# Feed-forward of a streaming encoder step as Strassen's seven block products

## Time and profile before

| | |
|---|---|
| time, median of 3 runs | 2838.29 us (2837.95 to 2841.03) |
| profiled execution, span | 2834.8 us |
| TensorE busy | 2717.8 us, 96% of the span, 18594 matmuls |
| VectorE busy | 1578.1 us, 56% |
| ScalarE busy | 1007.8 us, 36% |
| feed-forward matmuls L1857 | 6 groups of 768, 128x352 each, from 2081.47 us to the end of the span |

### The profile page before, as it was taken

How to read it: one execution, slowest core, us unless ns; L and a number is a source line. 1 busy time by engine, 2 the same in 40 slices (tenths; PEclk the granted TensorE clock), 3 DMA queues, 4 the chain that set the end, 5 groups by cost and what they waited for, 6 DMA issues and landing times. The chain is left out here.

```text
span 2834.8 us, 47428 instructions
## 1 busy us (share of the span) xinstructions
PE 2717.8 (96%) x18594; PEld 2642.7 (93%) x18594; DVE 1578.1 (56%) x2975; ACT 1007.8 (36%) x2302; POOL 207.6 (7%) x299
## 2 busy tenths in 40 slices
PE   5999989999999999989999989998989999999999
PEld 5999889999999999979999989998989999999999
DVE  5433536566566566557998845454363444444434
ACT  4333336556655656653343422112221111111110
POOL 0000000000000000004555510000000000000000
PEclk8999999999999999999999989999989999999999
DMA  4332353343343343328888854333221111111112
GB/s 161 122 122 76 107 156 101 96 124 101 90 128 104 90 134 97 92 84 193 210 200 211 203 157 141 120 121 125 70 89 45 45 45 45 45 47 54 50 56 97
DMA packets 326606, 308.72 MB, mean 109 GB/s; under 512 B 66480, under 2 KB 283056, under 8 KB 326256
## 3 DMA queue, kind: packets, MB, share of 16 engines
q1 hardware_dynamic: 326384, 305.69, 37.1%
HBM read 218.32 MB, written 87.28 MB: 108 GB/s over the span
## 5 line engine op out<-in xcount | busy, mean ns | idle before, releaser
L411 PE MATMUL banks<-w_hi,xn_hi 128*128 128x256 f32 x1440 | 408.3, 288 | 5.0 <-DVEq L368 5.0
L411 PE MATMUL banks<-w_lo,xn_hi 128*128 128x256 f32 x1440 | 403.4, 284 | 0.0
L414 PE MATMUL banks<-xn_hi,w_hi 128*128 128x352 f32 x1152 | 380.2, 330 | 11.9 <-ACTq L352 7.3
L414 PE MATMUL banks<-xn_hi,w_lo 128*128 128x352 f32 x1152 | 379.6, 330 | 0.0
L414 PE MATMUL banks<-xn_lo,w_hi 128*128 128x352 f32 x1152 | 379.3, 329 | 0.0
L411 PE MATMUL banks<-w_hi,xn_lo 128*128 128x256 f32 x1280 | 364.0, 284 | 0.0
L411 PEld LDWEIGHTS banks<-w_hi,xn_hi 128*128 128x128 f32 x1440 | 274.9, 191 | 6.6 <-DVEq L368 5.1
L411 PEld LDWEIGHTS banks<-w_lo,xn_hi 128*128 128x128 f32 x1440 | 274.5, 191 | 0.1
L1857 PE MATMUL banks<-h_hi,w_hi 128*128 128x352 f32 x768 | 248.9, 324 | 2.5 <-DVEq L1778 2.5
L1857 PE MATMUL banks<-h_hi,w_lo 128*128 128x352 f32 x768 | 248.7, 324 | 0.0
L1857 PE MATMUL banks<-h_lo,w_hi 128*128 128x352 f32 x768 | 248.7, 324 | 0.0
(11 more groups left out here) (282 smaller groups left out, 5903.2 us busy)
## 6 DMA issues: line engine op xcount, KB each, us to landing
w_raw<-in_w_in SPq DMA_DIRECT2D x44, 1024.0 KB, 5.9
scratch_xbc<-att_co SPq DMA_DIRECT2D x32, 512.0 KB, 2.9
ssd_ab<-scratch_acum SPq DMA_DIRECT2D x64, 256.0 KB, 5.9
br_g<-scratch_gates SPq DMA_DIRECT2D x72, 176.0 KB, 3.8
scratch_gates<-hand_tanh SPq DMA_DIRECT2D x48, 176.0 KB, 5.4
att_k<-scratch_k_hi SPq DMA_DIRECT2D x64, 128.0 KB
scratch_z<-att_z_stage SPq DMA_DIRECT2D x64, 128.0 KB, 2.0
ssd_xbc<-scratch_xbc SPq DMA_DIRECT2D x64, 128.0 KB, 3.4
```

The source lines that it names most:

```text
L411: ins = self.nc.tensor.matmul(self.bank(n, P, PW), x[:, k, t * P:(t + 1) * P], w[:, k, :], start=first, stop=end)
L414: ins = self.nc.tensor.matmul(self.bank(n, P, TT), w[:, k, m * P:(m + 1) * P], x[:, k, r * TT:(r + 1) * TT], start=first, stop=end)
```

Cut to its core:

```diff
+class DownSums:
+    CHUNKS, EVERY, ROWS = 8, 9, 2
+    def sp(self, sp, n):
+        c, step = n // self.EVERY, n % self.EVERY
+        if step == 0:
+            if c:
+                sp.wait_ge(self.stored, 64 * c)
...
+        elif step == 8:
+            sp.wait_ge(self.made, 4 * c + 4)
...
+    def dve(self, dve, n):
...
 def branches(...):
@@ block.sync
                 stream.sp(sp, 0, n, True)
+                down.sp(sp, n)
+            down.finish(sp)
@@ block.vector
                     make_lo(turn_at(n))
+                down.dve(dve, n)
 def out_norm(...):
-                        nc.scalar.activation(hi[:, blocks, cols], bank, ACT.Copy).then_inc(t_hi, 1)
+                            nc.scalar.activation(quarter(t // 4, i % 2)[:, :, t % 4 * P:(t % 4 + 1) * P], bank, ACT.Copy).then_inc(kept, 1)
-                        nc.vector.tensor_tensor(lo[:, blocks, cols], bank, hi[:, blocks, cols].bitcast(F32), ALU.subtract).then_inc(t_lo, 1)
 def mlp(...):
+    OPENING = [(0, 1), (1, 1), (0, 2), (1, 2), (0, 5), (0, 6), (0, 7), (0, 4), (0, 3), (1, 6), (1, 5), (1, 7), (1, 4), (1, 3)]
+    STEADY = [1, 6, 2, 7, 5, 4, 3]
+    order = OPENING + [(p, n) for p in range(2, PANELS) for n in STEADY]
+    DOWN = [1, 2, 6, 7, 4, 5, 3]
@@ block.sync
+            sp.wait_ge(d_lo, 2 * CHUNKS)
+            sp.dma_start(x2_last[:], x2_prompt[0:512, 512:D].rearrange("(t p) n -> p t n", p=P)).then_inc(last_loaded, 16)
+            for i in range(len(piece)):
+                load_x2(i)
@@ block.scalar
+            x_high(1); unit_high(0); unit_high(1); x_high(2); unit_high(2); unit_high(3)
+            x_high(5); keep_first(0); x_high(6); keep_first(1); x_high(7); take_c11(0)
+            x_high(4); take_c11(1); x_high(3)
...
@@ block.vector
+            for n in (5, 6, 7, 4):
+                t_sum(0, n)
+            x_low(1); unit_low(0); unit_low(1); x_low(2); unit_low(2); unit_low(3)
...
+            for i in range(FIRST, STEPS):
...
+            for q in range(CHUNKS):
+                if q + 2 < CHUNKS:
+                    down_low(q + 2)
+                if s == SL - 1 and 0 < i < len(DOWN) - 1:
+                    for f in range(FP):
+                        collect(i, f)
@@ block.tensor
+            def product(p, n):
+                pe.wait_ge(w_lo, i + 1)
+                pe.wait_ge(x_lo, made_at[n])
...
+                for a, (x, y, k) in enumerate(passes):
+                    for c in range(2):
+                        ins = nc.tensor.matmul(bank(slot_of(p, n), c), y[:, k, :], x[:, k, c * HC:(c + 1) * HC],
...
```

More of the change, by code:

```diff
@@ L1353, in branches @@
+def branches(core, handed, rms, gates, w_pa, w_pb, merged, following, w_down, t_d):
     nc = core.nc
@@ L1709, in _ @@
         @block.sync
         def _(sp):
[L1711 to L1723, removed]
@@ new lines, in store_last @@
+            def store_last(f):
+                sp.wait_ge(last_added, f + 1 if f < FP - 1 else FP + 1)
+                cols = slice(512 + f * P, 512 + (f + 1) * P)
+                sp.dma_start(y_prompt[0:512, cols].rearrange("(t p) n -> p t n", p=P), x2_last[:, :, f * P:(f + 1) * P]).then_inc(y_stored, 16)
+            load_up(1)
+            ready = {max(place[p, n] for n in (1, 2, 3)): p + 2 for p in range(PANELS - 2)}
+            for i, (p, n) in enumerate(order):
+                for unit in fresh.get(i, ()):
+                    if unit in ready:
+                        load_up(ready[unit])
+                if n == 3:
+                    store_early(p)
+                for pp, part in after.get(i - 1, ()):
+                    (store_late if part else store_sums)(pp)
+                if (p, n) == (PANELS - 1, 6):
+                    sp.wait_ge(up_done, done_at(PANELS - 1, 1))
+                    load_a(0)
+                    load_a(1)
+                    sp.wait_ge(w_lo, STEPS)
+                    load_b(0)
+                    load_b(1)
@@ L1744, in _ @@
+            sp.dma_start(y_running[0:TAIL_T, 512:D], x2_tail[:]).then_inc(y_stored, 16)
+            sp.wait_ge(y_stored, 16 * (len(piece) + FP + 1))
         @block.scalar
         def _(act):
[L1746 to L1761, removed]
-                            act.wait_ge(u_made, s * 2 * UP + j * UP + t + 1)
-                            nc.scalar.activation(relu[t % 2], core.banks[:, n % NB, 0:TT], ACT.Relu).then_inc(relued, 1)
-                    on, slot = items(j)
-                    if not (last and on):
-                        split(s + on, slot)
@@ new lines, in _ @@
+            x_high(1)
+            unit_high(0)
+            unit_high(1)
+            x_high(2)
+            unit_high(2)
+            unit_high(3)
+            x_high(5)
+            keep_first(0)
+            x_high(6)
+            keep_first(1)
+            x_high(7)
+            take_c11(0)
+            x_high(4)
+            take_c11(1)
+            x_high(3)
+            for i in range(FIRST, STEPS):
+                p, n = order[i]
+                for unit in fresh[i]:
+                    unit_high(unit)
+                if i > FIRST:
+                    pp, nn = order[i - 1]
+                    if nn in (4, 3) or (nn == 5 and pp >= 2):
+                        activate(pp, nn)
+                    elif nn == 7 and pp < 2:
+                        activate(pp, 5)
+                if n == 1:
+                    keep_first(p)
+                elif n == 2:
+                    take_c11(p)
+                if (p, n) == (PANELS - 1, 7):
+                    down_high(0)
+                elif (p, n) == (PANELS - 1, 3):
+                    down_high(1)
@@ new lines, in _ @@
+            x_low(6)
+            dve.wait_ge(s_made, 2)
+            dve.wait_ge(x_lo, made_at[2])
+            tensor(quarter[A12], quarter[A12], s2[:], ALU.subtract).then_inc(s_made, 1)
+            x_low(7)
+            x_low(4)
+            x_low(3)
+            for i in range(FIRST, STEPS):
+                for unit in fresh[i]:
+                    unit_low(unit)
+                for p, part in after.get(i, ()):
+                    (add_last if part else add_up)(p)
+                take(i)
+                if order[i] == (PANELS - 1, 5):
+                    down_low(0)
@@ new lines, in _ @@
+            for p, n in order:
+                product(p, n)
+            LAST = len(DOWN) - 1
+            for i in range(LAST):
+                for s in range(SL):
+                    for f in range(FP):
+                        down(i, s, f)
+            for f in range(FP):
+                for s in range(SL):
+                    down(LAST, s, f)
+                    if (f, s) in turns_after:
+                        turn(turns_after[f, s])
+                    if f and s == 1:
+                        turn_last(f - 1)
```

659 lines of the change are left out of this document (496 added, 163 removed).

## The result

The changed kernel takes **2807.5 us** in the median of four runs (2804.0 to 2816.3), the kernel before, beside it on the same chip, 2838.2 (2838.0 to 2841.0). The ratio is 0.9896 with a 95% interval of 0.988 to 0.9912: 1.0% faster, where 1.5% and 2796 us were forecast. The profiled execution has a span of 2802.2 us against 2834.8.

What follows compares the result with a forecast made beforehand. The feed-forward was taken to be bound by the number and spacing of TensorE's matmuls. Of 83 us gained there, half is given back to waits: span 2792.8 us, plus 3.5 for the median, gives 2796 us, range 2768 to 2822.

Steps and rivals of the forecast that it cites:

- part 1: Feed-forward: 4608 matmuls of 352 columns become 5376 of 264, spaced 0.1217 us; 83 us gained if TensorE never waits.
- The rule weighed against the change: Matmul spacing estimated from the Trainium skill: 110 ns at 352 columns, 99 at 264, so the change loses 23 us.
- part 2: Branches: loading, summing and storing w_down there costs 8 us, bounds 2 and 30; SyncE's store wait costed at nothing.
- branches and loads worse: Rival in the branches: rows of the turned operand arrive late at tiles 21 and 48, panels too; 2825 us, chance 0.13.
- The prediction's own sign of being wrong: Branches: the prediction counts as wrong if they grow by more than 15 us.
- The slower rival: Branches: gates behind SyncE's store wait stall TensorE; the 42 us gain gone at X = 30, 2852 us at 32; chance 0.04.
- X: Time of one chunk's stores in the branches; TensorE stalls from 24 us on, each us beyond costing seven.
- part 3: End of the output stage: low halves of the turned rows go, so the feed-forward block starts 6.2 us earlier.
- part 4: Opening of the up half: operands made in fixed order delay product (0,5) to 2118.2 us; later waits 2.7, clock 2.0.
- part 5: Steady state: no waits inside panels, but 3 us at the change of half and 9.6 at the last product.
- Change of half: Between up and down half: chunk 2 loads only after the last panel's stores; 3 us of wait, bounds 0 to 8.
- Last product: End of the down half: residual rows load late, TensorE waits 7.6 us, 2 more for the clock; bounds 0 and 15.

Runs made afterwards that it cites:

- the sums alone: Changed kernel with the w_down sums at their tiles, but one load of the first chunk and no stores: 2796.3 us, 0.985 of the kernel before.
- the last version: Changed kernel with reordered opening, residual loaded early, w_down sums and transfers moved clear of the turns, last stores at tile 69: 2784.2 us, 0.981 of the kernel before.

## Why the prediction came out as it did

The direction and the largest term were right: 31 of the 42 us came, and the time lay 11 us above the forecast and inside its own range. Most of the miss, 7 of the 11 us, is one term.

- **The matmuls (part 1): right.** Forecast 0.1217 us at 264 columns, measured 0.1218 and 0.1223. The run with 240 columns shows the line going on below the 256 of the earlier trace rows, slightly flatter. The rule weighed against the change does not hold here for this kind of matmul: by the two figures of the Trainium skill (TensorE: Matmul & The Clock Gate, Back-to-back issue gap) an estimate was 99 ns at 264 columns and 0.13 ns for each column more; the runs have 0.39 to 0.43.
- **The branches (part 2): the step that failed.** 8 us were put down, 14.5 came, and 0.8 more in the pause behind them. The text asked of SyncE's store wait what it does to the *gates*, which have four tiles and four banks of room, and "cost this at nothing". Behind the same wait stand the rows of the turned operand, fetched two tiles ahead of their use; they have no such room. SyncE's queue around the first turn, above, shows it: 8.3 us of wait, rows 5.3 us late, a pause of 4.6. The half that was costed, 3.5 and 3 us of new wait ahead of tiles 28 and 52, was right in its places and near in its sizes: the pauses grew from 1.18 us each to 2.61 and 4.89, by 1.4 and 3.7. But the size is luck, as the reason given for it, VectorE's own work, fell: with the sums alone the two pauses grew by 0.0 and 0.8. It is the late rows in front of that work that make them. The rival "branches and loads worse" had named the rows at tiles 21 and 48, at 0.13, and it is what happened, at 11 of its 29 us. The prediction's own sign of being wrong, branches that grow by more than 15 us, stayed off by 0.5 us in the profile of the changed kernel; in the three other profiles of the same code they grew by 16.1 to 17.8.
- **The slower rival** (SyncE's store wait, deciding from X = 24 us): a single store landed in 4.3 to 5.8 us in the median, and with the longest wait, 8.3 us, a chunk's four stores took 11.7 us from the first issue to the wait's end, far below the point.
- **The end of the output stage (part 3): right.** Its last transpose comes 6.5 us earlier, counted from the stage's start, where 6.2 were forecast. The first matmul of the feed-forward came 7.2 us after the forecast 2088.6, which is the miss of the branches.
- **The opening (part 4): right.** Forecast a pause of 10 to 14 us that ends with (0,5) 29.6 us after the first matmul; measured 3.70 and 9.95 us, the second ended 28.6 us after it. In order of time on TensorE (start us, us, instruction, idle before it and what ended that), the first row is product (0,2), which waits for the copy of product 1 behind operand 5, the second is (0,5):

```profile
2107.25 0.78 PE L2277 MATMUL banks<-mlp_xhi,mlp_ring_hi 128*128 128x264 f32 x2 [3.42 <-ACT mlp_r L1976]
...
2124.39 0.81 PE L2277 MATMUL banks<-mlp_xhi,mlp_ring_hi 128*128 128x264 f32 x2 [9.67 <-DVE mlp_ring_lo L2092]
```

 The waits behind their sums, put at 0.9 each, were 1.05 beyond the normal spacing.
- **The two ends of the down half (part 5): right.** Change of half: 2.83 us ahead of chunk 2, where 3 were forecast, and 1.57 ahead of the first down product, which was not in the sum. Last product: 7.77 where 7.6 were, ended by the load that was named, with the clock low behind it (order of time on VectorE, then on TensorE):

```profile
2747.51 1.35 DVE L2200 TENSOR_TENSOR mlp_x<-banks,mlp_x 128x512 f32<-128x512 f32 x2 [6.12 <-DMA mlp_x<-scratch_x]
```
```profile
2748.26 1.11 PE L2310 MATMUL banks<-ident,mlp_sum 128*128 128x128 f32 x4 [7.49 <-DVE mlp_x L2200]
2749.02 0.79 PE L2299 MATMUL banks<-mlp_a_hi,mlp_b_hi 128*128 128x264 f32 x2
```

 The tail is 7.0 us after the last matmul's start, forecast 6.4.
- **The sum.** First to last matmul of the feed-forward: forecast 697.8 (2088.6 to 2786.4), measured 699.4. So the span's 9.4 us over the forecast are 7.2 from the branches, 1.6 and 0.6 behind. The rest of the 11 is that the median now lies 5.3 us above the profiled span, where 3.5 was carried over.

The branches of the last version still take 3.5 us more than without `DownSums`. Its trace has two reasons: one pause of 1.76 us in the first turn, where SyncE issues the first rows 77.6 us after the start of the branches and not 70.5, and 29 matmuls at the lower clock against 19, 1.3 us. What stays open is why SyncE comes to those rows later there, and why rows land as late when the other transfers go through another queue.

## What to carry to other kernels

When a wait is put into a queue, list everything that stands behind it and ask for each how far ahead of its use it is issued; the tightest decides, not the most frequent. A load that comes late costs where the engine that uses it has no slack to catch up, so transfers that can go anywhere belong outside the stretches in which others are fetched just in time, and the last of them well before a block's end. And a gain by fewer columns is read off the spacing of two sizes in the same trace: here two rows gave it within half a per cent.

## What the runs showed that was not expected

- Transfers on a queue of their own slow the others as much as on the same queue: 512 KB of rows landed in 8.0 us with `DownSums` on GpSimd's queue, 8.2 on SyncE's, 5.3 without it. VectorE's waits for them fell all the same, from 20.3 to 13.3 us.
- A pause costs more than its length: in the branches matmuls of 352 columns at the lower granted clock (one every 0.29 us) were 21 before and 37 after the change, which is 2.8 and 4.9 us beside the pauses themselves.
- From 264 to 240 columns the spacing fell by 0.39 to 0.41 ns a column, a little less than from 352 to 256 (0.434).
